# Three pads before the activation buffers of a one-core decoder layer: their start addresses modulo 256 bytes against those of the split weights

## The chip, the cores and the metric

The kernel runs on one core of one Trainium2 chip. The metric is the device time of one execution in microseconds (us). TensorE multiplies, VectorE (DVE), ScalarE (ACT) and GpSimd (POOL) work element by element, SyncE (SP) only issues transfers here. SBUF is the on-chip memory of 128 partitions; a buffer takes the same byte range in every partition, and "address" below means the byte offset in a partition. TensorE reads both operands of a product from SBUF: the stationary one (the weights, 128x128) by a weight load, the moving one (the activations, 128 x up to 512 columns) during the matmul itself.

## The reference

One decoder layer on x of 256 tokens by 2048 channels, all in float32:

```
h = rms_norm(x);  proj = h @ w_in                      # 10240 columns
o_a = hgrn2(...); o_b = s5(...); o_c = stick_breaking(...)
merged = sum_k sigmoid(gate_k) * (o_k @ w_branch[k]);  x = x + merged @ w_out
up = causal_depthwise_conv(rms_norm(x) @ w_up, conv_w)
x = x + (silu(up[..., :D_FF]) * up[..., D_FF:]) @ w_down    # D_FF = 5632
```

Every large product has 256 tokens as its moving columns and weights that are read once.

## The kernel before

**Work on TensorE.** Each large product goes by blocks of 128x128 weights. For accuracy each weight is split into a high part (`w_hi`, written by ScalarE from the raw weights, line 740) and a low part (`w_lo` = raw minus high, by VectorE, line 1065), and each activation likewise into a high part (index 0) and a low part (index 1) of one buffer. The product is high x high + high x low + low x high. There are two ways to issue it:

- as a pair (`piece`, lines 373 and 375): one matmul of 512 columns, the high weights against both parts of the activation, and one of 256 columns, the low weights against the high part. This is done for the first 8 tiles of the input projection (moving buffer `a_raw`), the GLU product (`glu_in`), the output projection (`a_in`, filled anew with the merged branches), the up projection (`h2`) and the down projection (`act`) but for its last tile.
- as a triple (`in_piece` line 387, `plain_piece` line 398, `branch_piece` line 413): three matmuls of 256 columns. This is done for the other 72 tiles of the input projection (8 tiles with `a_raw`, 64 with `a_in`), the branch products (`o_hg`, `o_sb`, `o_s5`, named `o_s` in the trace) and the last down tile.

Each tile's sums go to one of four PSUM banks. Between tiles of the input projection stand the small products of the three mixers (`mixers`, lines 432 to 569), among them `within` (lines 540 and 543): moving `softp_hi` and `softp_lo`, stationary `lower` and `ones`.

**Order.** Each engine has its own written program; semaphores tie them. SP loads raw weights into a ring of 4 buffers `raw`, ScalarE and VectorE split them into rings of 4 `w_hi` and 4 `w_lo` buffers of 4096 bytes each, TensorE uses them.

**Addresses.** Buffers are handed out one behind the other in the order of the `sb` calls, each rounded up to 32 bytes. `raw`, `w_hi` and `w_lo` come first, so that every one of them starts at 0 modulo 256; each block of 128 weights in them is 512 bytes long and so starts at 0 modulo 256, too. Behind them come constants, and the last of these is a pad:

```
        sb("apart", [P, 40])
```

It is 160 bytes long and ends at byte 58656, which is 32 modulo 256. There two sets of buffers begin that share the same bytes at different times: `early` (`a_in`, `x_first`, `a_raw`, `gates`, the mixers' buffers, `o_hg` and so on) and `late` (`act`, `x1`, `h2`, `sum_u`, `padded`, `convd`, `silu`). The sizes of the activation buffers are whole multiples of 256 bytes, and each 256-token row in them is 1024 bytes, so every moving operand of a large product starts at 32 modulo 256: its distance from the weights is 32 bytes everywhere. `lower` starts at 32 modulo 256 and `ones` at 0, so of the `within` products those with `lower` have the distance 0, and those with `ones` the distance 32.

Of the kernel before, what the change touches and what calls it, by code (L numbers as in the profile page):

```python
# [38 lines left out]
F32 = mybir.dt.float32  # L39
# [6 lines left out]
P = 128  # L46
# [88 lines left out]
def layer(nc, xT, w_in, w_glu, w_br, w_out, w_up, w_down, norm_mix, norm_ffn, hg_gain, s5_small, s5_b, s5_c,  # L135
          s5_skip, sb_gain, conv, out):
    ctx = ExitStack()
    with ctx:
        def sb(name, shape, dt=F32, scope=None):
            return (scope or ctx).enter_context(nc.sbuf_tensor(name, shape, dt))  # L140
# [25 lines left out]


        late = ExitStack()
        act = sb("act", [P, FT, 2, SEQ], F32R, late)
        x1 = sb("x1", [P, KT, SEQ], F32, late)  # L170
        h2 = sb("h2", [P, KT, 2, SEQ], F32R, late)
        sum_u = sb("sum_u", [P, 2, SEQ], F32, late)
        padded = sb("padded", [P, 2, SEQ + 2], F32, late)
# [3 lines left out]


        early = ExitStack()
        a_in = sb("a_in", [P, KT, 2, SEQ], F32R, early)  # L180
        head = ExitStack()
        x_first = sb("x_first", [P, KT, SEQ], F32, head)
# [1618 lines left out]
```

## Time and profile before

| What | Value |
|---|---|
| median of 3 runs | 1395.51 us (1395.27 to 1395.55) |
| the profiled execution, its own time | 1395.73 us |
| its span, first to last instruction | 1394.1 us |
| TensorE busy | 1389.1 us of the span |
| VectorE, ScalarE, GpSimd busy | 1031.5, 751.1, 142.8 us |
| granted TensorE clock, mean | 1.0 of full speed (2.4 GHz) |
| read from HBM | 258.66 MB, 187 GB/s over the span |

The profile is of one execution; 1.6 us of its own time lie outside the span. A matmul's duration in a row is longer than the distance between two starts, since matmuls overlap in the array. The pace is read from distances between starts, or from the busy time of a group that covers a stretch without a gap, divided by the count.

### The profile page before, as it was taken

To read this page: it belongs to the slowest core of one execution; us is meant where nothing else is said; L and a number is where in the kernel's file an instruction comes from. 1 tells how busy PE (TensorE), PEld (TensorE's weight loads), DVE (VectorE), ACT (ScalarE), POOL (GpSimd) and SP (SyncE) were. 2 spreads that over 40 slices of the span, in tenths; PEclk is the share of its full clock that TensorE was granted. 3 is DMA by queue.
4 is the path that set the end of the run, shared out by engine and by line. 5 is a ranking of instruction groups with operands and counts; after the bars stand their busy time and mean duration, and the time that the engine had idled before them with its cause. 6 is when DMAs were issued, how large, how long until landed. Compare 5 with 4: busy or idle time off the path is not lost.

```text
span 1394.1 us, 27849 instructions
## 1 busy us (share of the span) xinstructions
PE 1389.1 (100%) x9854; PEld 1281.7 (92%) x9854; DVE 1031.5 (74%) x1425; ACT 751.1 (54%) x1053; POOL 142.8 (10%) x187
## 2 busy tenths in 40 slices
PE   9999999999999999999999999999999999999999
PEld 8999999999999999988888888888888888888888
DVE  7999857799888677776687777777777775445453
ACT  7575676844544454554655555555555554344432
POOL 1200000000000024322111111111111110000000
PEclk9999999999999999999999999999999999999999
DMA  8655545446555556756565655566566556666663
GB/s 285 188 185 180 181 154 181 144 160 194 172 194 167 188 175 223 229 182 195 169 209 183 194 191 185 182 196 192 185 193 192 184 176 196 209 188 200 194 207 108
DMA packets 76513, 261.70 MB, mean 188 GB/s; under 512 B 8800, under 2 KB 10368, under 8 KB 76448
## 3 DMA queue, kind: packets, MB, share of 16 engines
q1 hardware_dynamic: 74304, 255.89, 57.6%
q0 software_dynamic: 1424, 4.37, 1.1%
q8 instruction: 46, 0.75, 0.2%
q10 hardware_dynamic: 720, 0.53, 0.1%
q14 instruction: 19, 0.16, 0.0%
HBM read 258.66 MB, written 2.10 MB: 187 GB/s over the span
## 4 chain that ended last, share of the span: by engine, by line
PE 98%; ACT 1%; DMA 1%; DVE 0%; SPq 0%; issue 0%; ACTq 0%
PE bank L373 40%; PE bank L387 29%; PE bank L375 21%; PE bank L413 5%; PE pair L432 1%; PE bank L398 1%; DMA x_first<-xT 0%; PE pair L569 0%; DMA raw<-w_in 0%; ACT w_hi L740 0%; ACT gates L750 0%; PE pair L438 0%; SPq L295 0%; PE pair L540 0%; ACT L750 0%
## 5 line engine op out<-in xcount | busy, mean ns | idle before, releaser
L1065 DVE TENSOR_TENSOR w_lo<-raw,w_hi 128x1024 fp32r<-128x1024 f32 x496 | 584.7, 1189 | 297.7 <-ACT w_hi L740 293.4
L740 ACT ACTIVATE w_hi<-raw 128x1024 fp32r<-128x1024 f32 x496 | 508.8, 1030 | 418.9 <-PE bank L375 200.1
L373 PE MATMUL bank<-h,w_hi 128*128 128x512 f32 x1408 | 488.4, 390 | 0.0
L375 PE MATMUL bank<-h,w_lo 128*128 128x256 f32 x1408 | 397.1, 282 | 0.0
L387 PE MATMUL bank<-a_in,w_hi 128*128 128x256 f32 x2048 | 363.5, 281 | 0.0
L387 PEld LDWEIGHTS bank<-a_in,w_hi 128*128 128x128 f32 x2048 | 312.0, 188 | 4.1 <-issue 3.6
L373 PEld LDWEIGHTS bank<-h,w_hi 128*128 128x128 f32 x1408 | 264.2, 188 | 55.4
L387 PE MATMUL bank<-a_in,w_lo 128*128 128x256 f32 x1024 | 285.5, 279 | 0.0
L375 PEld LDWEIGHTS bank<-h,w_lo 128*128 128x128 f32 x1408 | 266.1, 189 | 0.0
L373 PE MATMUL bank<-act,w_hi 128*128 128x512 f32 x660 | 228.8, 390 | 0.0
L387 PEld LDWEIGHTS bank<-a_in,w_lo 128*128 128x128 f32 x1024 | 192.5, 188 | 0.0
L375 PE MATMUL bank<-act,w_lo 128*128 128x256 f32 x660 | 186.1, 282 | 0.0
L373 PEld LDWEIGHTS bank<-act,w_hi 128*128 128x128 f32 x660 | 123.8, 188 | 26.0
L375 PEld LDWEIGHTS bank<-act,w_lo 128*128 128x128 f32 x660 | 124.7, 189 | 0.0
L1725 POOL TENSOR_TENSOR padded<-sum_u,rstd 128x256 f32<-128x256 f32 x88 | 73.8, 839 | 413.3 <-DVE sum_u L1086 400.4
L373 PE MATMUL bank<-a_in,w_hi 128*128 128x512 f32 x256 | 88.8, 390 | 0.0
L375 PE MATMUL bank<-a_in,w_lo 128*128 128x256 f32 x256 | 72.2, 282 | 0.0
L1005 ACT ACTIVATE silu<-convd 128x256 f32<-128x256 f32 x43 | 17.9, 417 | 96.1 <-DVE convd L1585 96.1
L1583 DVE SCALAR_TENSOR_TENSOR convd<-padded,taps,convd 128x256 f32<-128x256 f32 x88 | 62.7, 713 | 1.0 <-ACT convd L1025 1.0
L1585 DVE SCALAR_TENSOR_TENSOR convd<-padded,taps,convd 128x256 f32<-128x256 f32 x88 | 54.0, 613 | 11.5
L373 PEld LDWEIGHTS bank<-a_in,w_hi 128*128 128x128 f32 x256 | 48.0, 188 | 10.0
L747 ACT ACTIVATE half<-bank 128x256 f32<-128x256 f32 x135 | 49.2, 365 | 3.8 <-PE bank L375 3.7
(230 smaller groups left out, 1358.1 us busy)
## 6 DMA issues: line engine op xcount, KB each, us to landing
raw<-w_up SPq DMA_DIRECT2D x176, 512.0 KB, 3.7
raw<-w_in SPq DMA_DIRECT2D x156, 512.0 KB, 4.2
raw<-w_down SPq DMA_DIRECT2D x80, 512.0 KB, 4.3
raw<-w_out SPq DMA_DIRECT2D x32, 512.0 KB, 4.2
raw<-w_br SPq DMA_DIRECT2D x16, 512.0 KB, 3.6
raw<-w_br SPq DMA_DIRECT2D x16, 256.0 KB, 3.3
raw<-w_down SPq DMA_DIRECT2D x16, 256.0 KB, 2.7
x_first<-xT SPq DMA_DIRECT2D x8, 256.0 KB, 6.3
```

The costliest lines, as they stand in the source:

```text
L373: pe.matmul(bank[b][:, :], w[:, k * P:(k + 1) * P], a.rearrange("p a t -> p (a t)"), start=first and n == 0, stop=False, skip_group_check= ...
L375: mm = pe.matmul(bank[b][:, 0:SEQ], l[:, k * P:(k + 1) * P], a[:, 0, :], start=False, stop=last and n == len(blocks) - 1, skip_group_check ...
L387: mm = pe.matmul(bank[n % BANKS][:, 0:SEQ], x[:, k * P:(k + 1) * P], src[:, PIECE * h + k, part, :], start=h == 0 and k == 0 and m == 0, s ...
L398: mm = pe.matmul(bank[b][:, 0:SEQ], x[:, k * P:(k + 1) * P], rhs(k, part), start=first and k == 0 and m == 0, stop=last and k == blocks - ...
L413: mm = pe.matmul(bank[b][:, 0:SEQ], x[:, cols], src[:, k, part, :], start=k == 0 and m == 0, stop=k == CT - 1 and m == 2, skip_group_check ...
L740: act_e.activation(w_hi[s][:, 0:blocks * P], raw[s][:, 0:blocks * P], ACT.Copy).then_inc(hi_ready, 1)
L747: act_e.activation(half[j % 2][:, :], bank[j % BANKS][:, SEQ:2 * SEQ], ACT.Copy).then_inc(half_copied, 1)
L1005: act_e.activation(silu[:, :], convd[:, (j - 3) % 4, :], ACT.Silu).then_inc(S("silu_done"), 1)
L1065: ve.tensor_tensor(w_lo[s][:, w], raw[s][:, w], w_hi[s][:, w].bitcast(F32), ALU.subtract).then_inc(lo_ready, 1)
L1583: ve.scalar_tensor_tensor(c, padded[:, j % 2, 1:SEQ + 1], taps[:, t, 1:2], c, ALU.mult, ALU.add).then_inc(S("tap1"), 1)
L1585: ve.scalar_tensor_tensor(c, padded[:, j % 2, 0:SEQ], taps[:, t, 0:1], c, ALU.mult, ALU.add).then_inc(S("conv_done"), 1)
L1725: pool.tensor_tensor(padded[:, j, 2:], sum_u[:, j, :], rstd[:, :], ALU.mult).then_inc(S("up_scaled"), 1)
```

## The change

Three pads are added. `apart_act` (160 bytes) stands before `act`, `apart_h2` (32 bytes) before `h2`, and `apart_in` (224 bytes) before `a_in`. Nothing else is changed: each engine has the same instructions in the same order (their line numbers are up to 3 higher).

```
         late = ExitStack()
+        sb("apart_act", [P, 40], F32, late)
         act = sb("act", [P, FT, 2, SEQ], F32R, late)
         x1 = sb("x1", [P, KT, SEQ], F32, late)
+        sb("apart_h2", [P, 8], F32, late)
         h2 = sb("h2", [P, KT, 2, SEQ], F32R, late)
...
         early = ExitStack()
+        sb("apart_in", [P, 56], F32, early)
         a_in = sb("a_in", [P, KT, 2, SEQ], F32R, early)
```

By adding up sizes, the start addresses modulo 256 become:

| Buffer, and where it is the moving operand | before | after |
|---|---|---|
| `a_raw`, `a_in` (input projection) | 32 | 0 |
| `o_hg`, `o_sb`, `o_s5`, `glu_in` (branches, GLU) | 32 | 0 |
| `a_in` (output projection) | 32 | 0 |
| `h2` (up projection) | 32 | 224 |
| `act` (down projection) | 32 | 192 |
| `softp_hi`, `softp_lo` against `lower` / `ones` | 32 - 32 = 0 / 32 | 0 - 32 = 224 / 0 |
| `x1`; `sum_u`, `padded`; `convd`, `silu` (not read by TensorE) | 32; 32; 64 | 192; 224; 0 |
| `raw`, `w_hi`, `w_lo` | 0 | 0 |

## Rows read from the trace of the kernel before

**Rows 1.** The page: its head, the engines' busy time, the granted clock in 40 slices
```profile
span 1394.1 us, 27849 instructions
...
PE 1389.1 (100%) x9854; PEld 1281.7 (92%) x9854; DVE 1031.5 (74%) x1425; ACT 751.1 (54%) x1053; POOL 142.8 (10%) x187
...
PEclk9999999999999999999999999999999999999999
```

**Rows 2.** The page: the chain that ended last, by engine
```profile
PE 98%; ACT 1%; DMA 1%; DVE 0%; SPq 0%; issue 0%; ACTq 0%
```

**Rows 3.** Groups by line: matmuls; busy us and mean ns of one
```profile
L373 PE MATMUL bank<-h,w_hi 128*128 128x512 f32 x1408 | 488.4, 390 | 0.0
L375 PE MATMUL bank<-h,w_lo 128*128 128x256 f32 x1408 | 397.1, 282 | 0.0
...
L373 PE MATMUL bank<-act,w_hi 128*128 128x512 f32 x660 | 228.8, 390 | 0.0
...
L373 PE MATMUL bank<-a_in,w_hi 128*128 128x512 f32 x256 | 88.8, 390 | 0.0
...
L373 PE MATMUL bank<-glu_in,w_hi 128*128 128x512 f32 x32 | 11.1, 390 | 0.0
```

**Rows 4.** The timeline, TensorE in the up projection: start us, duration us
```profile
1000.06 0.28 PE L375 MATMUL bank<-h,w_lo 128*128 128x256 f32 x1
1000.18 0.39 PE L373 MATMUL bank<-h,w_hi 128*128 128x512 f32 x1
1000.41 0.28 PE L375 MATMUL bank<-h,w_lo 128*128 128x256 f32 x1
```

**Rows 5.** The timeline, weight loads of the same stretch
```profile
1000.18 0.19 PEld L375 LDWEIGHTS bank<-h,w_lo 128*128 128x128 f32 x1
1000.41 0.19 PEld L373 LDWEIGHTS bank<-h,w_hi 128*128 128x128 f32 x1
```

**Rows 6.** The chain in order of time: start us, length us, what
```profile
375.10 39.77 PE bank L387 x336
...
422.76 39.77 PE bank L387 x336
...
502.83 67.20 PE bank L413 x576
```

**Rows 7.** Windows for line 387: stretch, us; TensorE busy us (count)
```profile
376.50:415.50 39.00, 38.38 (x326) 38.17 (x325) 1.00 0.57 187
```

**Rows 8.** The timeline, the `within` products on TensorE
```profile
262.95 0.39 PE L540 MATMUL pair<-softp_hi,lower 128*128 128x512 f32 x1
263.18 0.40 PE L540 MATMUL pair<-softp_lo,lower 128*128 128x512 f32 x1
263.42 0.28 PE L540 MATMUL pair<-softp_hi,lower 128*128 128x256 f32 x1
...
263.89 0.40 PE L540 MATMUL pair<-softp_hi,lower 128*128 128x512 f32 x1
264.13 0.40 PE L540 MATMUL pair<-softp_lo,lower 128*128 128x512 f32 x1
264.36 0.28 PE L540 MATMUL pair<-softp_hi,lower 128*128 128x256 f32 x1
264.47 0.28 PE L540 MATMUL pair<-softp_lo,lower 128*128 128x256 f32 x1
```

**Rows 9.** The waits: who waited for whom, us in total, times, longest
```profile
DVE w_lo L1065 <- ACT w_hi L740: 293.4, 258, 5.9
ACT w_hi L740 <- PE bank L375: 200.1, 190, 2.1
```

**Rows 10.** Windows, all engines, up projection: PE, PEld, DVE, ACT, POOL
```profile
1000.00:1100.00 100.00, 100.00 (x578) 88.63 (x578) 77.96 (x109) 56.07 (x90) 15.13 (x18) 1.00 0.60 190
```

**Rows 11.** The page: the first input transfer, KB each, us to landing
```profile
x_first<-xT SPq DMA_DIRECT2D x8, 256.0 KB, 6.3
```

More of the change, by code:

```diff
@@ L168, in layer @@
         late = ExitStack()
+        sb("apart_act", [P, 40], F32, late)
         act = sb("act", [P, FT, 2, SEQ], F32R, late)
         x1 = sb("x1", [P, KT, SEQ], F32, late)
+        sb("apart_h2", [P, 8], F32, late)
         h2 = sb("h2", [P, KT, 2, SEQ], F32R, late)
@@ L179, in layer @@
         early = ExitStack()
+        sb("apart_in", [P, 56], F32, early)
         a_in = sb("a_in", [P, KT, 2, SEQ], F32R, early)
```

## The prediction

> **What bounds the kernel now.** I read the page's list of engines first: TensorE is busy for 1389.1 us of a span of 1394.1 us, at full clock in every slice [rows 1]. The chain of work that ended last is then hardly news: 98% of it is TensorE [rows 2]. The waits say the same from the other side: ScalarE's split waits for TensorE to release a weight buffer (200.1 us in all), and VectorE's split waits for ScalarE (293.4 us) [rows 9]. In the up projection VectorE is busy for 77.96 of 100 us and ScalarE for 56.07 [rows 10]. Nobody feeds TensorE too late, but for a few microseconds at the head. So only one thing can move the time by more than a microsecond: the distance between the starts of two matmuls inside an unbroken run of them.
>
> That distance comes from the groups by line. The 512-column matmuls of the up projection overlap one another without a gap, so their busy time divided by their count is the time of a pair (512 + 256 columns): 488.4 us / 1408 = 346.9 ns. The down projection gives 228.8 / 660 = 346.7, the output projection 88.8 / 256 = 346.9, the GLU product 11.1 / 32 = 346.9 [rows 3]. The granted clock is at the 2.4 GHz level, at which 768 columns, one a cycle, would be 320 ns. So 27 ns of each pair, 7.7%, are something else than columns. The branch products, in triples of 256, take 67.20 / 576 = 116.7 ns each, 350.0 ns for the same 768 columns, against 320 again [rows 6]. The timeline shows what runs beside: a weight load of 0.19 us begins with each matmul, for the next one [rows 4, 5]. In any stage one stream reads activations from SBUF while another reads weights. If the extra 27 to 30 ns are partly collisions of the two, the relative address could matter. If they are a fixed cost of changing weights, it can't.
>
> **Is there anything in the trace that varies at a fixed distance?** Yes, and it is my main evidence. In the input projection, with the same code, buffer and distance, runs of triples go at two paces. A window inside one run of line 387 holds 326 matmuls in 38.38 us, 117.7 ns each or 353.2 ns a triple [rows 7]; the branch runs hold 350.0 [rows 6]. The long runs of 336 in the chain have 39.77 / 336 = 118.4 ns, a little of it the restart at their head [rows 6]. A cost that was fixed by the instruction would not have two values. So some of the extra depends on how the streams stand to each other in time, and an address offset shifts just that. The step between the two paces, 353.2 - 350.0 = 3.2 ns per 768 columns, is the unit I calculate with.
>
> **The change part by part.**
>
> Instructions: none are added, removed or moved, on any engine or queue. No wait is added. All that is to be priced is the residue of addresses.
>
> 1. `h2` from 32 to 224, up projection: 1408 pairs [rows 3]. No row has a moving operand at 224. Above: the `within` products have the distance 0, the other side of 32; four starts of 512-column matmuls there lie 0.47 us apart two by two (262.95 to 263.42, 263.89 to 264.36), 0.235 us each [rows 8], against about 0.229 in the pair (0.3469 less the 0.12, here taken as 0.118, between 1000.06 and 1000.18 [rows 4]): 6 ns more per pair, +8.4 us. Below: a 256-column matmul can start its successor after 0.11 us (264.36 to 264.47) [rows 8] rather than 0.118, 8 ns less per pair, -11.3 us. I take one unit less, 3.2 ns, as the size of the step that the trace shows to exist: 1408 x 3.2 = -4.5 us.
> 2. `act` to 192, down projection: 660 pairs. The same reasoning, between +4.0 and -5.3 us; taken 660 x 3.2 = -2.1 us. Its last tile is 132 matmuls in triples, below 0.2 us.
> 3. `a_raw` and `a_in` to 0, input projection: 3456 matmuls of 256 columns in 1152 triples (72 tiles of 16 blocks). The runs of 336 and several shorter ones, about half of all, are in the slow pace. If the new distance keeps them all in the fast one: 576 x 3.2 = -1.8 us. If it puts all in the slow one: +1.8 us. If 0.11 us were held, 1152 x 3 x 6.7 ns = -23 us. I take -1.8 us.
> 4. Distance 0 also for the 128 pairs of the first tiles, the 32 of the GLU product and the 256 of the output projection, together 416 pairs. The `within` rows say +6 ns, 2.5 us; one unit would be -1.3 us. The `within` rows are the first matmuls of a run, where the pace may not be settled. I take 0. For the 576 branch matmuls, already at the fast pace, also 0.
> 5. What VectorE, ScalarE, GpSimd and the transfers do with buffers at other residues: VectorE has 22% of the up projection to spare [rows 10], which hides any slowing below that; where the cover ends is the head, with x arriving 6.3 us after issue [rows 11]. It is 224 bytes further in each partition; between -0.5 and +0.5 us, taken as 0.
>
> Sum: -4.5 - 2.1 - 1.8 = -8.4 us on the profiled execution's 1395.7 us (span 1394.1 and 1.6 around it), 1387.3 us. The median of the runs is 0.2 us below that execution: 1387.1, forecast as 1387. What is late next is still TensorE: at a pair of 343.6 ns the 16 weight blocks of a tile take about 5.5 us, and VectorE's 22% is far from used up.
>
> The page "TensorE: Matmul & The Clock Gate" of the Trainium skill, section "Wait — 56ns, not 53.3ns?", gives N / 2.4 GHz plus about 2.5 ns between starts. By it a pair would be 325 ns; the trace has 346.9, so this kernel pays some 11 ns a matmul that the page's figure does not have [rows 3].
>
> **Rivals.**
>
> A. Nothing moves. The two paces are set by when a run starts, and an address does not enter: the two reads never meet, and the extra is the price of changing the weights. For it: pairs agree to 0.2 ns in four buffers [rows 3]. Against it: this agreement is among buffers that all stand at 32, so it says nothing on other distances; and the two paces at line 387 need something that meets. Time: 1395.7 less the 0.2 = 1395.5 us. The same page of the Trainium skill, section "Step-by-step: what each phase is for", states just this mechanism: two independent read ports, so that loading the next weights takes nothing from the running matmul. That the trace has two paces for one code speaks against the strict form of it; no run here has yet moved an address.
>
> B. Slower. The streams meet as I think, but 32 was on the good side, and 0, 224 and 192 are on the bad one. Place: each pair in its 512-column matmul, which has the weight load in its first part. Price: the 6 ns of the `within` rows, at a distance of 0. 2484 pairs (1408 + 660 + 416) x 6 = +14.9 us, and all triples of the input projection in the slow pace, +1.8: 1395.5 + 16.7 = 1412.2 us. It decides as soon as the mean cost per pair is over 1.1 ns. For it: 0 is the one other distance that the trace has, and it reads slower there [rows 8]. Against: those are eight matmuls at the head of a run and after other shapes. A mixed form (only the stages at 0 lose, up and down stay) gives +2.5 + 1.8 = 1399.8 us.
>
> C. A larger gain. The collisions are most of the extra, and the new distances let them fall into the gap between matmuls. Then 256-column matmuls reach the 0.11 us at least every other time, as in the `within` rows: half of 2068 x 8 ns and of 3456 x 6.7 ns is -19.9 us, and with one unit of 3.2 on the pairs' 512 columns -6.6: 1369 us.
>
> **How the numbers follow.** Forecast (a gain between 3 and 16 us): 0.40. A: 0.18. B and its mixed form: 0.30. C: 0.12. Time 1387 us, its own range 1380 to 1392. For 8 in 10 the range must take in A, most of B and most of C: 1369 to 1410 us. The difference that a measurement of this kernel can tell is about 0.2%, 2.8 us. Faster 0.52 (forecast and C), same 0.18 (A), slower 0.30 (B).
>
> **What would show it.** In the profile of the changed kernel the busy time of the 512-column matmuls on `h`, over 1408, should be near 343.6 ns, that on `act`, over 660, too: 346.9 means rival A, 350 or more rival B, below 341 rival C. Up and down have the same pattern of reads and differ only in 224 against 192, so different paces in the two would show that each 32 bytes matter. The runs of 336 on line 387 should take 39.3 rather than 39.77 us. The output projection, pairs at distance 0, tells a cost of 0 from one of 224. The forecast would be wrong in its root if all these are unchanged, and wrong in sign if 32 was a good place. If these paces stay and the time still moves, it is the head or a wait that I priced at nothing.

## The result, and the profile after

The changed kernel takes 1422.65 us (median of 4 runs, 1422.04 to 1423.35) against 1395.53 us before in the same comparison: the ratio is 1.0193, 95% interval 1.0181 to 1.0205. It is 27 us slower. The forecast was 1387 us, a gain.

The page of the changed kernel has the same instructions, the same clock and a busier TensorE: head, engines, granted clock, and the chain by engine.

```profile
span 1421.7 us, 27849 instructions
...
PE 1416.7 (100%) x9854; PEld 1291.3 (91%) x9854; DVE 1032.8 (73%) x1425; ACT 751.6 (53%) x1053; POOL 142.9 (10%) x187
...
PEclk9999999999999999999999999999999999999999
...
PE 98%; DMA 1%; SPq 0%; ACT 0%; DVE 0%; issue 0%
```

TensorE is busy for 27.6 us more, which is the whole of the span's growth (1394.1 to 1421.7); VectorE, ScalarE and GpSimd have the same work within 1.3 us [rows 1, 2]. So the time went into the distance between the starts of matmuls, as the prediction said it must. The groups by line (busy us, mean ns of one), to be read against [rows 3]:

```profile
L376 PE MATMUL bank<-h,w_hi 128*128 128x512 f32 x1408 | 497.8, 397 | 0.0
...
L376 PE MATMUL bank<-act,w_hi 128*128 128x512 f32 x660 | 233.2, 397 | 0.0
...
L376 PE MATMUL bank<-a_in,w_hi 128*128 128x512 f32 x256 | 90.5, 399 | 0.0
```

Busy over count gives 353.6 ns a pair in the up projection, 353.3 in the down and 353.5 in the output projection, against 346.9, 346.7 and 346.9. These are means. Before the change the unbroken pairs of the up projection take 346 or 347 ns, all but one; after it, pairs of 346 and 361 ns take turns. The timeline, from one 512-column start to the next:

```profile
999.62 0.39 PE L376 MATMUL bank<-h,w_hi 128*128 128x512 f32 x1
...
999.96 0.40 PE L376 MATMUL bank<-h,w_hi 128*128 128x512 f32 x1
...
1000.32 0.39 PE L376 MATMUL bank<-h,w_hi 128*128 128x512 f32 x1
...
1000.67 0.40 PE L376 MATMUL bank<-h,w_hi 128*128 128x512 f32 x1
```

The chain in order of time (start us, length us, what) answers to [rows 6]:

```profile
382.63 40.50 PE bank L390 x336
...
431.15 40.50 PE bank L390 x336
...
512.95 69.11 PE bank L416 x576
...
1403.61 15.56 PE bank L401 x132
```

A branch matmul takes 69.11 / 576 = 120.0 ns instead of 116.7, and a run of 336 input matmuls 40.50 instead of 39.77 us. The window of the up projection (PE, PEld, DVE, ACT, POOL, with counts) has 569 instead of 578 matmuls in 100 us, and VectorE has more time to spare, not less [rows 10]:

```profile
1000.00:1100.00 100.00, 100.00 (x569) 86.84 (x568) 77.07 (x107) 55.23 (x89) 14.53 (x18) 1.00 0.59 186
```

The stages follow each other without a gap, so the first starts give their lengths. These are the rows of lines 376 and 390 of the changed kernel (duration ns min/median/max, first and last start us):

```profile
L376 PE MATMUL bank<-h,w_hi x1408: 392/396/581, 672.4 to 1169.9; 128*128 128x512 f32 x176
L376 PE MATMUL bank<-act,w_hi x660: 388/397/398, 1170.3 to 1403.1; 128*128 128x512 f32 x165
L376 PE MATMUL bank<-a_in,w_hi x256: 395/398/403, 581.9 to 672.0; 128*128 128x512 f32 x128
...
L376 PE MATMUL bank<-glu_in,w_hi x32: 395/398/403, 501.5 to 512.4; 128*128 128x512 f32 x32
...
L390 PE MATMUL bank<-a_in,w_hi x2048: 277/283/389, 102.7 to 501.2; 128*128 128x256 f32 x187
...
L390 PE MATMUL bank<-a_raw,w_hi x256: 277/283/466, 53.9 to 101.7; 128*128 128x256 f32 x128
```

With the same starts in the kernel before (52.9, 100.7, 491.6, 569.9, 658.6, 1147.2 us):

| Stage | distance, before and after | us before | us after | difference |
|---|---|---|---|---|
| head and first pairs, up to the first triple | 32, 0 | 52.9 | 53.9 | +1.0 |
| input triples on `a_raw` | 32, 0 | 47.8 | 48.8 | +1.0 |
| input triples on `a_in`, mixers' products included | 32, 0 | 390.9 | 398.8 | +7.9 |
| GLU and branches | 32, 0 | 78.3 | 80.4 | +2.1 |
| output | 32, 0 | 88.7 | 90.5 | +1.8 |
| up | 32, 224 | 488.6 | 497.9 | +9.3 |
| down and the rest | 32, 192 | 246.9 | 251.4 | +4.5 |

These add up to 27.6 us.

### The profile page after: what moved, and what is told of

It is laid out like the page before. It is cut to its first block, busy times and chain, and to the rows that moved or that the text cites. A ratio compares the mean times of both kernels' runs of the same rounds, so it can differ in the third digit from the quotient of the medians.

```text
span 1421.7 us, 27849 instructions
## 1 busy us (share of the span) xinstructions
PE 1416.7 (100%) x9854; PEld 1291.3 (91%) x9854; DVE 1032.8 (73%) x1425; ACT 751.6 (53%) x1053; POOL 142.9 (10%) x187
## 4 chain that ended last, share of the span: by engine, by line
PE 98%; DMA 1%; SPq 0%; ACT 0%; DVE 0%; issue 0%
PE bank L376 40%; PE bank L390 29%; PE bank L378 21%; PE bank L416 5%; PE pair L435 1%; PE bank L401 1%; DMA x_first<-xT 0%; PE pair L572 0%; DMA raw<-w_in 0%; PE pair L441 0%; SPq L298 0%; PE pair L543 0%; SPq L318 0%; DVE w_lo L1068 0%; ACT w_hi L743 0%; ACT a_raw L901 0%
## 5 line engine op out<-in xcount | busy, mean ns | idle before, releaser
L376 PE MATMUL bank<-h,w_hi 128*128 128x512 f32 x1408 | 497.8, 397 | 0.0
L390 PE MATMUL bank<-a_in,w_hi 128*128 128x256 f32 x2048 | 371.7, 284 | 0.0
L390 PEld LDWEIGHTS bank<-a_in,w_hi 128*128 128x128 f32 x2048 | 319.0, 192 | 3.9 <-issue 3.4
L390 PE MATMUL bank<-a_in,w_lo 128*128 128x256 f32 x1024 | 289.7, 283 | 0.0
L376 PE MATMUL bank<-act,w_hi 128*128 128x512 f32 x660 | 233.2, 397 | 0.0
L390 PEld LDWEIGHTS bank<-a_in,w_lo 128*128 128x128 f32 x1024 | 196.4, 192 | 0.0
L376 PE MATMUL bank<-a_in,w_hi 128*128 128x512 f32 x256 | 90.5, 399 | 0.0
L378 PE MATMUL bank<-a_in,w_lo 128*128 128x256 f32 x256 | 71.9, 281 | 0.0
L1588 DVE SCALAR_TENSOR_TENSOR convd<-padded,taps,convd 128x256 f32<-128x256 f32 x88 | 53.9, 612 | 11.5
L376 PEld LDWEIGHTS bank<-a_in,w_hi 128*128 128x128 f32 x256 | 48.1, 188 | 11.9
```

The costliest lines, as they stand in the source:

```text
L376: pe.matmul(bank[b][:, :], w[:, k * P:(k + 1) * P], a.rearrange("p a t -> p (a t)"), start=first and n == 0, stop=False, skip_group_check= ...
L378: mm = pe.matmul(bank[b][:, 0:SEQ], l[:, k * P:(k + 1) * P], a[:, 0, :], start=False, stop=last and n == len(blocks) - 1, skip_group_check ...
L390: mm = pe.matmul(bank[n % BANKS][:, 0:SEQ], x[:, k * P:(k + 1) * P], src[:, PIECE * h + k, part, :], start=h == 0 and k == 0 and m == 0, s ...
L1588: ve.scalar_tensor_tensor(c, padded[:, j % 2, 0:SEQ], taps[:, t, 0:1], c, ALU.mult, ALU.add).then_inc(S("conv_done"), 1)
```

## The experiments

Where a pace to a tenth of a nanosecond stands here, it is the mean distance of starts in the trace, over all pairs or triples of a stage that no wait breaks (single ones can differ from it, as above). Runs with one measurement are compared with a run of the kernel before on the same chip; the paces come from their traces. Two theories stood at the start. D: the pace goes by the distance modulo 256 between the moving operand and the split weights. L: 32 is the one good place. Two rivals were to be excluded: that the residue of the moving buffer alone decides, and that a stage does.

**Other distances, in steps of 32.** The pads are the only edit.

```
+        sb("apart_act", [P, 24], F32, late)     # 128; before h2: 56 (96); before a_in: 8 (64)
```

> Distances 64 (input, branches, GLU, output), 96 (up) and 128 (down) instead of 32. Theory D: the pace is set by the distance modulo 256 between moving operand and split weights, because the two reads meet in SBUF; every distance has its own pace. Then pairs here lie anywhere from 340 to 355 ns and differ between output (64), up (96) and down (128). Theory L: 32 is one lucky value and all others cost the same, 353.3 to 353.6 ns a pair and 120.0 ns a 256-column matmul of a triple, as 0, 192 and 224 do: then the time is 1422 us again. Theory N (a near neighbour of 32 is as good): output pairs at 64 stay at 347, the others at 353.

1408.37 us against 1396.08. Pairs: 353.3 ns in the output projection (64), 350.0 in the up (96), 351.1 in the down projection (128). Input triples at 64 are at 353.0 ns on average. D holds; L falls, and so does N (64 is no better than 0).

```
+        sb("apart_act", [P, 16], F32, late)     # 96; before h2: 8 (128); before a_in: 32 (160)
```

> Distances 160 (input, branches, GLU, output), 128 (up) and 96 (down). Together with the kernel that has 96 in the up and 128 in the down projection this crosses two distances over two stages. Theory D: the pace of a pair goes with the distance and not with the stage, to within 0.3 ns. If the stage decides (its other engines, its transfers), the up projection has one pace at 96 and at 128. Theory L: 1422 us again.

1408.56 us. Up at 128 has 351.1 ns and down at 96 has 350.0: the paces changed places with the distances. The stage has no part in it. Output pairs at 160 have 346.7 ns, the same as at 32, so 32 is not alone. Input triples at 160: 354.3 ns.

**Is it the distance or the place?** Every buffer moved by 192 bytes:

```
+        sb("shift", [P, 48])
         raw = [sb(f"raw{s}", [P, PIECE * P]) for s in range(RING)]
...
+        sb("apart_act", [P, 64], F32, late)
```

> Every buffer, weights included, is moved by 192 bytes, so all distances are 32 as in the kernel before, while the moving buffers start at 224 modulo 256, where the changed kernel has the up projection; act is moved by 256 bytes more. Theory D (only the distance counts, modulo 256): 346.9 ns a pair in every stage, 1395.5 us, within 0.2%. Rival: the residue of the moving operand by itself decides: 353.6 ns a pair in the up projection, about 1420 us. If the period is longer than 256 bytes, the down projection alone changes its pace from 346.7 ns.

1396.05 us against 1396.08. Pairs are at 346.7 ns in all stages. Its groups for the up and down pairs read as before, digit for digit:

```profile
L375 PE MATMUL bank<-h,w_hi 128*128 128x512 f32 x1408 | 488.4, 390 | 0.0
...
L375 PE MATMUL bank<-act,w_hi 128*128 128x512 f32 x660 | 228.8, 390 | 0.0
```

Then the counterpart, the weights alone moved by 96 bytes, with no activation buffer touched:

```
+        sb("apart_w", [P, 24])
         w_hi = [sb(f"w_hi{s}", [P, PIECE * P], F32R) for s in range(RING)]
...
-        sb("apart", [P, 40])
+        sb("apart", [P, 16])
```

> Only the split weights move, by 96 bytes; every activation buffer stays where it is in the kernel before, at 32. All distances become 32 - 96, which is 192 modulo 256. Theory D: every pair at 353.3 ns and every triple at about 353.3 ns, as the down projection had them at 192; 2484 pairs x 6.7 and 192 branch triples x 3.3 and 1152 input triples x 1.7 give 1395.5 + 16.6 + 0.6 + 2.0 = 1415 us. If it were the activation buffers' own residue, or something of the vector engines and transfers on them, nothing moves: 1396 us.

1406.35 us against 1395.84. Its groups have the pair at 497.8 / 1408 and 233.2 / 660, which is the changed kernel's 353.3 in the down projection:

```profile
L374 PE MATMUL bank<-h,w_hi 128*128 128x512 f32 x1408 | 497.8, 397 | 0.0
...
L374 PE MATMUL bank<-act,w_hi 128*128 128x512 f32 x660 | 233.2, 397 | 0.0
```

So a distance makes the pace of pairs, whichever side is moved: all 2484 pairs lost their 6.7 ns as foretold (16.6 us). But the total was 9 us better than expected, and the chain says where:

```profile
371.97 38.30 PE bank L388 x336
...
418.19 38.30 PE bank L388 x336
...
457.48 28.46 PE bank L388 x240
...
497.25 67.84 PE bank L414 x576
```

The runs of 336 input matmuls take 38.30 us, not 39.77: at 192, input triples have two paces, 340.0 and 353.3 ns, with a mean of 344.6 on `a_in` (on `a_raw`, at the same distance, 351.8, nearly all in the slow pace). The branches at the same distance are all at 353.3 (67.84 / 576 = 117.8 ns). I had not expected this; the last experiment uses it.

One rival is left by these two kernels: that the moving read meets not the read of the next weights but the writes of ScalarE and VectorE, which put the split weights into the same buffers. The trace of the changed kernel speaks against it. In its up projection, 274 of 1406 unbroken pairs overlap no instruction that writes `w_hi` or `w_lo`, and 42 pairs of the down projection overlap no instruction of VectorE, ScalarE or GpSimd at all; both sets have 353.3 ns, like the others.

**One part alone.** Only the pad before `a_in`.

```
+        sb("apart_in", [P, 56], F32, early)
         a_in = sb("a_in", [P, KT, 2, SEQ], F32R, early)
```

> Only the pad before a_in: distance 0 in input, branches, GLU and output, 32 in up and down as before. If the parts add up, stage by stage: up and down give back 9.4 + 4.6 of the 27 us, so 1408.5 us, with 120.0 ns per matmul of a triple and 353.3 ns per output pair, and 346.7 ns in up and down. If a part works through a neighbour (transfers or splits that fall late), the sum is another and up is not at 346.7.

1409.3 us against 1396.11: +13.2, where the stages of the changed kernel at distance 0 gave 13.8 (1.0 + 1.0 + 7.9 + 2.1 + 1.8). Up and down are at 346.7 ns. The parts add up.

**Is it the meeting of two reads?** Half the weight columns in up and down:

```
-                    pe.matmul(bank[b][:, :], w[:, k * P:(k + 1) * P], a.rearrange("p a t -> p (a t)"),
+                    pe.matmul(bank[b][0:cols, :], w[:, k * P:k * P + cols], a.rearrange("p a t -> p (a t)"),
```

> In the up and down projections each weight load and each matmul takes only the first 64 of a block's 128 weight columns (half of the sums of these two stages are left out); up at distance 224, down at 32. The moving columns are the same. Theory M (the extra is the moving read meeting the read of the next weights): with half as long a weight load there is half as much to meet, so the extra over 320 ns falls clearly, from 27 ns (down, 32) and 33 ns (up, 224) to about 13 to 20 ns, and the 6.7 ns between the two distances shrink or vanish. Theory F (a fixed price of each change of weights, with the distance acting on something else, for instance on the moving read alone): 346.7 and 353.3 ns stay as they are.

```profile
L374 PE MATMUL bank<-h,w_hi 128*64 128x512 f32 x1408 | 493.7, 396 | 0.0
...
L374 PEld LDWEIGHTS bank<-h,w_hi 128*64 128x64 f32 x1408 | 188.9, 134 | 138.7
...
L374 PE MATMUL bank<-act,w_hi 128*64 128x512 f32 x660 | 228.9, 392 | 0.0
```

A weight load takes 134 instead of 188 ns. At 224 the pair falls from 353.3 to 350.5 ns; at 32 it stays at 346.7. So there are two parts. The part that the distance adds shrinks with the weight load, from 6.7 to 3.8 ns: that fits a meeting of the moving read with the read of the next weights. It does not prove it, since half the columns of weights also mean half the results written to PSUM. The 26.7 ns over 320 that remain at the best distance did not change. What theory M expected came true for the first part and not for the second.

**Which weights?** High and low weights at different places (low ones 32 or 128 bytes further):

```
+        sb("apart_lo", [P, 8])      # the other kernel: 32
         w_lo = [sb(f"w_lo{s}", [P, PIECE * P], F32R) for s in range(RING)]
```

> The low weights start at 32 modulo 256, the high ones stay at 0. Distances to high and low weights: output 32 and 0, up 0 and 224, down 64 and 32. While the 512-column matmul runs, the next low weights are loaded, so by theory M the distance to the low weights sets its time and the distance to the high weights that of the 256-column one; a pair with one good distance (32) costs between 346.7 and 353.3 ns: output about 350, down about 350, up 353 or more. If only the distance to the high weights counts (the operand that the 512-column matmul itself uses), output stays at 346.7 and down at 353.3.

1397.59 us against 1396.11. Output (32 to the high, 0 to the low weights) 346.7 ns, up (0 and 224) 346.7, down (64 and 32) 348.9. Neither of the two forms expected has all three.

> The low weights start at 128 modulo 256, the high ones at 0. Distances to high and low: output and input 32 and 160, up 160 and 32, down 0 and 128. By theory M 32 and 160 are both good for a pair (346.7 ns), so output and up stay at 346.7 or fall below if the two places add up better than one distance alone can; down 352 to 353. If input triples fall below 350.0 ns, a faster kernel is to be had.

1403.09 us. Output (32 and 160) 346.7 ns, up (160 and 32) 346.7, down (0 and 128) 346.7; input triples (32 and 160) 356.6. Output and up are as expected, down is not. In both kernels a combination of two places that are bad alone (0 and 224, 0 and 128) has the mean of the good place, and no sum rule holds. Within the up pair of the first kernel the 512-column matmul takes 231.7 and the other 115.0 ns, instead of 228.3 and 118.3: the two matmuls shift time between them and the sum stays. The output pairs, with the same two places as the first tiles' pairs, are at 346.7 ns, the first tiles' 121 pairs at 345.2: the only mean below 346.7 ns in any kernel. In the input triples it is the other way round: two distances good for pairs make the worst of the multiples of 32 but 0 and 96.

**The part that no distance removes.** The low matmul left out in up and down.

```
+                        mm = pe.matmul(bank[b][:, :], w[:, k * P:(k + 1) * P], a.rearrange("p a t -> p (a t)"),
+                                       start=first and n == 0, stop=last and n == len(blocks) - 1, skip_group_check=True)
+                        continue
```

> In the up and down projections the matmul with the low weights is left out (and so that product): a run of 512-column matmuls only, up at distance 224, down at 32. Theory M adds the extra of the distance per weight load that meets a matmul: 224 costs about half of a pair's 6.7 ns more than 32, 3 to 5 ns per matmul, or 8 to 10 if only the load under a 512-column matmul meets it. For the part that no distance removes: if a matmul costs 17/16 of its columns plus 3.3 ns (which gives 346.7 ns a pair and 350.0 a triple), down is at 230.0 ns; if it costs 13/12 of its columns, 231.1 ns; if it is 13.3 ns a matmul, 226.7.

1300.44 us; TensorE now waits 107.4 us for VectorE's splits, so only the distances inside unbroken runs count. They are 233.1 ns a matmul at 224 and 233.3 at 32, 213.3 being the columns at 2.4 GHz. The timeline shows it, a row of 12 at 224 and one of 11 at 32 (start us, length us):

```profile
999.68 2.96 PE L375 MATMUL bank<-h,w_hi 128*128 128x512 f32 x12
...
1199.66 2.73 PE L375 MATMUL bank<-act,w_hi 128*128 128x512 f32 x11
```

Less the last matmul's own 0.39 to 0.40 us, that is 11 and 10 distances of 0.233 us. None of the three formulas fits, and the distance makes no difference in a run of 512-column matmuls only, where theory M expected 3 ns or more. So what the distance costs needs the alternation of long and short matmuls, or short ones; M in its simple form (so much for each load that meets a matmul) does not hold. What the remaining part is stays open.

**Below 32 bytes.** Views with an offset inside their buffer:

```
+        act = sb("act", [P, FT * 2 * SEQ + 8], F32R, late)[:, 2:2 + FT * 2 * SEQ].rearrange("p (k a t) -> p k a t", a=2, t=SEQ)
```

> Distances 224 (input, branches, GLU, output), 48 (up) and 40 (down), the last two between the steps of 32 bytes. Theory D with a unit of 32 bytes or more: 48 and 40 act as 32 (346.9 ns a pair) or as 64. Theory D with a finer unit: another pace than both. If what counts is that an operand starts on a multiple of 32 bytes, 40 and 48 are clearly slower than 353 ns. Input triples at 224: 120.0 ns each by theory L, anything from 116 to 121 by D.

1411.7 us. 48 has 350.0 ns, 40 has 353.3, and 224 in the output projection 353.3; input triples at 224 have 355.0. So 8 bytes beside the good place the whole 6.7 ns are back.

> Distances between the steps of 32: a_in (most of the input projection, output) 36, up 24, down 16; the first 16 input tiles at 64. If the good place at 32 is narrow, as 40 (353.3 ns) suggests, pairs at 24 and 16 cost 350 to 353.3 ns; if it is one-sided, 16 or 24 stay at 346.7. No distance is expected below 346.7, as two good distances (32, 160) share that number. Input triples at 36: 351.6 ns at 32, so anything from 350.0 (always the fast pace, a gain of about 1.5 us) to 360.

1423.93 us against 1395.84. 36 costs 356.7 ns a pair and 363.2 a triple, 24 costs 355.6; both are worse than any multiple of 32. 16 costs 346.7 a pair, and the last down tile at 16 takes 14.97 us for 132 matmuls, 340.0 ns a triple:

```profile
384.33 40.88 PE bank L389 x336
...
1404.81 14.97 PE bank L400 x132
```

> Distances 20 (most of the input projection, output), 12 (up), 8 (down), around 16. If the good place is as narrow as 36 and 24 make it look, all are slower than at 16: pairs 350 to 356 ns, input triples 350 to 363 ns. If only multiples of 16 are good because a moving read then starts on a line of its own, 8 is between.

1417.52 us. 12 gives 346.7 ns a pair, 8 gives 353.3, 20 gives 355.5 and 366.7 a triple, the slowest of all.

> Distances 176 (most of the input projection, output), 144 (up), 208 (down): the odd multiples of 16. 160 and 32 share the pace of a pair, 346.7 ns, so if the pattern repeats after 128 for pairs, 144 is at 346.7 as 16 is. Triples at 176 anywhere from 340.0 (16) to 354 (160). A pair below 346.7 ns at any of the three would show that 346.7 is no floor.

1406.86 us. 144 gives 346.7 ns, 176 and 208 give 350.0. 16 and 144, 32 and 160 agree: good places for pairs repeat after 128 bytes, while 0 (353.3) and 128 (351.1), 96 (350.0) and 224 (353.3) do not agree. The 346.7 at 144 is again a mean: single pairs there go round 343, 357 and 340 ns. So it is the mean over a stage that never fell below 346.7 at one distance, not each pair. Input triples at 176: 357.8.

**Sixteen bytes for all?** The weights 16 bytes later, nothing else moved:

```
+        w_all = sb("w_all", [P, 2 * RING * PIECE * P + 8], F32R)
+        w_hi = [w_all[:, 4 + s * PIECE * P:4 + (s + 1) * PIECE * P] for s in range(RING)]
...
-        sb("apart", [P, 40])
+        sb("apart", [P, 32])
```

> The split weights start 16 bytes later and every activation buffer stays, so that all distances are 16. Theory D with the paces read so far at 16 (346.7 ns a pair over 660 pairs, 340.0 ns a triple over 44 triples): pairs as before, 192 branch triples 10.0 ns less each and 1152 input triples 11.6 ns less each, 1.9 + 13.4 us, hence 1380.5 us, 1.1% faster than before. Rival: the input projection has its triples at 344.6 ns (as at distance 192), for restarts between tiles upset the pace: 1385.5 us. Rival: weights on a multiple of 16 only slow the splits on ScalarE and VectorE, and TensorE waits for them: over 1395.5 us.

1416.58 us, ratio 1.0148 (1.0131 to 1.0165). Pairs are at 353.3 ns at distance 16 with the weights shifted, where they are at 346.7 with the moving buffer shifted. TensorE does not wait for the splits; the pace itself is slower. So theory D does not hold below 32 bytes. There is one exception in this trace: the pairs of the GLU product, which have the same residues of weights and moving operand, take 346.7 ns, all 31 distances of them, and so do ten pairs in a row in the first tile of the input projection. So a pair as well can go at two paces at the same residues.

```
+        act = sb("act", [P, FT * 2 * SEQ + 64], F32R, late)[:, 4:4 + FT * 2 * SEQ].rearrange("p (k a t) -> p k a t", a=2, t=SEQ)
```

> Weights 16 bytes later; act and h2 16 bytes later, too, so that their distance is 32; the rest at distance 16 with weights at 16. If the distance alone decides, up and down are at 346.7 ns a pair. If the weights' own place within 32 bytes counts as well, they are at another pace, as the pairs at distance 16 were (353.3 with weights at 16, 346.7 with weights at 0).

1415.92 us: with both sides 16 bytes later and the distance back at 32, the up and down pairs stay at 353.3 ns (the GLU pairs, at distance 16, are at 346.7 again). With the weights on a multiple of 32, the 2065 up and down pairs at distance 32 in the kernel before take 346 or 347 ns, all but one. So the weights' own place within 32 bytes counts; whether it sets the pace or only decides which of two paces a run falls into is not shown.

```
+        sb("apart_in", [P, 56], F32, early)
+        a_in = sb("a_in", [P, KT * 2 * SEQ + 8], F32R, early)[:, 4:4 + KT * 2 * SEQ].rearrange("p (k a t) -> p k a t", a=2, t=SEQ)
```

> The weights stay at their place and the moving buffers a_in and act start 16 bytes behind it; a_raw, h2, the branch and GLU operands stay at 32. If the pace at 16 belongs to a moving buffer at 16 with weights at 0 (the last down tile: 340.0 ns a triple, the down pairs 346.7), 1024 input triples take 340.0 instead of 351.6 ns, 11.9 us less, the last down tile 0.4 us less: 1383 us, 0.9% faster than before. If the odd restart between tiles throws the input projection into a slow pace as at 36 and 20 (363 to 367 ns): up to 1410 us.

1396.46 us, ratio 1.0003 (0.9994 to 1.0012): no change. Pairs at 16 hold 346.7 ns. The input triples at 16 have three paces by tile, about 340, 350 and 356 ns, mean 353.8; the 340.0 of the last down tile is only one of them.

**A kernel faster than both.** `a_in` alone at 192, everything behind it at 32 again:

```
+        sb("apart_in", [P, 40], F32, early)
         a_in = sb("a_in", [P, KT, 2, SEQ], F32R, early)
+        sb("apart_rest", [P, 24], F32, early)
```

> Only a_in moves, to distance 192 (160 bytes before it, 96 behind it, so that everything after it is again at 32). With the weights moved by 96 the runs of 336 input matmuls took 38.3 instead of 39.8 us, and the mean triple of the input projection 344.6 instead of 351.6 ns. If the distance alone does that: 1024 triples x 7.0 ns, -7.1 us; the 256 output pairs on the same buffer lose 6.7 ns each, +1.7 us; the rest stays: 1390.1 us, 0.4% faster than before. If the pace of a triple depends on when a tile starts as much as on the distance, other restarts may put more of the runs at 353.3 ns: up to 1398.5 us.

1390.49 us, ratio 0.9961 (0.9947 to 0.9975): 5.1 us faster than the kernel before, with 5.4 expected. Its chain:

```profile
371.30 38.30 PE bank L389 x336
...
417.52 38.30 PE bank L389 x336
...
496.37 67.20 PE bank L415 x576
```

Input triples are at 343.6 ns on average (340.0 in three of four), the branches at 350.0 as before; the output pairs on the same buffer pay their 6.7 ns. The run of the branches starts at 496.37 instead of 502.83 us, and the output projection gives 1.8 us of that back.

All mean paces at distances measured with the weights at their own place (moving operand shifted), or, for 192, also with the weights shifted by 96:

| distance | pair, ns | triple, ns |
|---|---|---|
| 0 | 353.3 | 359.9 |
| 8, 12 | 353.3, 346.7 | 353.8 (last down tile), none |
| 16 | 346.7 | 340.0 (last down tile), 353.8 (input) |
| 20, 24 | 355.5, 355.6 | 366.7, none |
| 32 | 346.7 | 350.0 (branches), 351.6 (input) |
| 36, 40 | 356.7, 353.3 | 363.2, 357.8 (last down tile) |
| 48, 64 | 350.0, 353.3 | none, 353.0 to 353.3 |
| 96, 128 | 350.0, 351.1 | 359.9, 356.0 (last down tile) |
| 144, 160 | 346.7, 346.7 | none, 352.0 (branches), 354.3 (input) |
| 176, 208 | 350.0, 350.0 | 357.8, 357.5 (last down tile) |
| 192 | 353.3 | 353.3 (branches), 343.6 and 344.6 (input, `a_in`), 351.8 (input, `a_raw`) |
| 224 | 353.3 | 355.0 |

One correction to the tables ahead of the prediction: residues there are counted from the first weight buffer. The allocator's own addresses are 16,512 bytes higher, which adds 128 to each residue. Distances are not touched by it.

## Why the prediction was wrong

**Right:** that TensorE's pace between matmuls is the only thing that can move the time; that the pace depends on how the two reads stand to each other; that nothing on other engines moves; and the way to read all this off (busy over count on `h`, runs of 336). The marks set in "What would show it" answered plainly: 353.6 on `h` is rival B, whose mark was 350 or more.

**Step 1 and 2, the sign.** "I take one unit less, 3.2 ns": the size of a step was known from the two paces of the input projection, the direction was not. It was -4.5 and -2.1 us; measured are +9.3 and about +4.4. This is the step that failed: a change of distance was priced as a gain for the pairs, and it cost each of them 6.7 ns.

One reading in the prediction pointed to a loss: four 512-column starts at distance 0, 0.235 us each [rows 8]. I set it aside for being at the head of a run. The value looks right: after the change the 512-column matmul of a pair takes 235.0 ns in the down projection (192) and 236.7 in the output projection (0). But the `within` rows did not show an effect of the distance. In the changed kernel the same products have the distance 224 and take 0.47 us for two again:

```profile
268.34 0.40 PE L543 MATMUL pair<-softp_hi,lower 128*128 128x512 f32 x1
268.58 0.40 PE L543 MATMUL pair<-softp_lo,lower 128*128 128x512 f32 x1
268.81 0.28 PE L543 MATMUL pair<-softp_hi,lower 128*128 128x256 f32 x1
```

And at distance 32, in the kernel without the low matmul, a 512-column matmul behind another one starts after 233.3 ns, too. The 0.235 us belong to that order, long behind long, at each of the three distances. So rival B had its price of 6 ns from a row that did not measure it, and the agreement with 6.7 is luck, as far as these runs show.

The forecast's sign rested on nothing but that 27 ns of a pair looked like room. The runs show that 26.7 of them are there at every distance tried: 346.7 is the lowest mean of a stage's pairs over 19 distances and six mixed ones, but for the 345.2 of the first tiles in one mixed case. The kernel before was at the bottom for pairs, and of the distances tried none could win there.

**Step 3, the size.** The bound above for the input triples was "If it puts all in the slow one: +1.8 us." It took the two paces at distance 32 for the whole scale. At distance 0 a triple takes 359.9 ns, and the stage lost 8.9 us (1.0 + 7.9). Rival B with 16.7 us had 14.9 for the pairs, 16.6 being right, and 1.8 for the input where 8.9 belong; for the branches, 1.9 more. Step 4 (0 taken for 416 pairs and the branches) lost about 2.8 and 1.9 us. The range had a fault of its own: it was said to take in most of B, and it ended at 1410 us, below the 1412.2 that B was priced at.

**Rivals.** A falls by all runs: the pace of a pair goes by the distance between the two operands, whichever side is shifted, so the two reads act on each other. The sentence of the Trainium skill's page "TensorE: Matmul & The Clock Gate", section "Step-by-step: what each phase is for", that loading the next weights does not take from the running matmul, is contradicted here for the float32r operands of this kernel: the distance alone moves a pair by 6.7 ns, and by 3.8 ns when a load takes 134 instead of 188 ns. B was right in sign and place, and by luck in the price of a pair. C is excluded for pairs at the distances tried; for triples it has a kernel of truth, 340.0 against 350.0 ns, at distances that the change did not choose for them.

**What stays open.** Why 26.7 ns a pair remain; by what rule the two reads hinder each other, as neither mixed distances nor runs of long matmuls follow a sum; why the same distance gives triples two or three paces, and pairs two when the weights are 16 bytes off (which one a tile falls into may go by when it starts, which was not tried); why at some distances long and short pairs take turns; why the weights' place within 32 bytes matters.

## What to carry to other kernels

When TensorE streams both operands from SBUF and weights change with every matmul, measure start-to-start distances first, and treat the address distance between the two operands as a setting to be swept: here it is worth -0.4% to +2%, and neighbouring values 4 to 8 bytes apart differ by as much as distant ones. A gap to the ideal rate is not room for a particular knob; only a second setting of the knob shows that, so ask for one before you forecast a sign. Sweep pairs and triples (each order of matmuls) apart: the best place of one is not that of the other, and buffers can have different ones.

## What the runs showed of the hardware

- With the weights on multiples of 32 bytes, the pace of pairs goes by the distance of the operands and not by their place: 1396.05 against 1396.08 us with everything moved by 192 bytes.
- At multiples of 16 bytes the mean of a pair is 346.7, 350.0 or 353.3 ns, but for 351.1 at 128; the steps of 3.33 ns are 8 cycles at 2.4 GHz. Between the multiples of 16 there are 355.5 to 356.7 ns as well (20, 24, 36).
- The mean can hide a rhythm: pairs of 346 and 361 ns take turns at 224, and at 144 pairs of 343, 357 and 340 ns have the mean of 346.7.
- A triple on one buffer can hold either of two paces for a whole run at the same distance: 340.0 or 353.3 ns at 192.
- Halving the columns of the weight load (188 to 134 ns) lowers the pair at 224 from 353.3 to 350.5 ns and leaves the pair at 32 at 346.7.
- A run of 512-column matmuls with a weight load each takes 233 ns a matmul at 32 and at 224 alike.
- The 353.3 ns of a pair are the same with and without a write to the weight buffers by another engine beside it (1132 and 274 pairs).
